# Two-block model at sequence 512: work moved ahead of waits in three stages, and the last product written out in column halves

## The reference, cut to what matters

```python
# second block; the first block (chunked attention, convolution, gates) comes before it
h = h + mixer_ab(rmsnorm(h))                     # layer 0: sparse attention and gated linear attention
h = h + square(relu(rmsnorm(h) @ w_up[0])) @ w_down[0]
h = h + mixer_c(rmsnorm(h))                      # layer 1: stick-breaking attention
h = h + square(relu(rmsnorm(h) @ w_up[1])) @ w_down[1]

def mixer_c(n):                                  # 8 heads of width 128
    q, k, v = split(n @ w_in, (1024, 1024, 1024))
    q, k = rmsnorm(q) * gq, rmsnorm(k) * gk
    return stick_breaking(q, k, v) @ w_out

def stick_breaking(q, k, v):
    z = q @ k.T * d ** -0.5                      # mask: key earlier than query
    lo = where(mask, log_sigmoid(-z), 0)
    rc = cumsum(lo, reversed)
    a = where(mask, exp(log_sigmoid(z) + rc - lo), 0)
    return a @ v
```

## Time and profile before

| | |
|---|---|
| median of 3 runs | 1573.76 us (1573.63 to 1574.47) |
| profiled execution, whole | 1573.52 us |
| profiled execution, first to last instruction (span) | 1571.7 us |
| TensorE busy | 1557.9 us, 99% |
| VectorE busy | 1033.1 us, 66% |
| ScalarE busy | 725.2 us, 46% |
| GpSimd busy | 682.2 us, 43% |
| memory traffic | 92 GB/s over the span |

### The profile page before, as it was taken

One profiled execution on the slowest core, in us unless ns is written; L12 is line 12 of the kernel. 1 busy time (PEld: TensorE's weight loads), 2 busy tenths in 40 slices (PEclk: granted clock), 3 DMA queues, 4 the chain that ended last, 5 costly groups with the idle time before them and its releaser, 6 DMA issues.

```text
span 1571.7 us, 20555 instructions
## 1 busy us (share of the span) xinstructions
PE 1557.9 (99%) x7578; PEld 1279.2 (81%) x7578; DVE 1033.1 (66%) x1342; ACT 725.2 (46%) x1086; POOL 682.2 (43%) x668
## 2 busy tenths in 40 slices
PE   9999999999999999999999999999999999999999
PEld 7888787788778998788888888887887888888887
DVE  7424554674688977558484857878777557575848
ACT  6323433325245565345353535476765453444433
POOL 0002110104345453286675748353333484857564
PEclk9999999999999999999999999999999999999999
DMA  7232222232221221422323131222121314141421
GB/s 247 81 107 80 80 80 80 96 107 80 85 76 55 70 79 57 159 81 103 112 80 135 56 134 53 81 81 81 54 81 45 144 54 161 54 161 54 137 78 54
DMA packets 25731, 145.07 MB, mean 92 GB/s; under 512 B 3936, under 2 KB 5680, under 8 KB 9264
## 3 DMA queue, kind: packets, MB, share of 16 engines
q1 hardware_dynamic: 25648, 143.95, 26.5%
HBM read 141.84 MB, written 2.10 MB: 92 GB/s over the span
## 4 chain that ended last, share of the span: by engine, by line
PE 83%; DVE 11%; ACT 3%; issue 1%; POOL 1%; DVEq 0%; ACTq 0%; POOLq 0%
PE ps_G L614 19%; PE ps_G L616 18%; PE ps_G L615 18%; PE ps_C L1274 5%; PE ps_C L1276 5%; PE ps_C L1275 5%; DVE wide L2666 1%; DVE top L2662 1%; PE ps_AV L1103 1%; PE ps_AV L1274 1%; PE ps_AV L1276 1%; PE ps_AV L1275 1%; DVE wide L2858 1%; PE ps_C L713 1%; DVE tmp L2295 1%
## 5 line engine op out<-in xcount | busy, mean ns | idle before, releaser
L614 PE MATMUL ps_G<-ch,wh 128*128 128x512 f32 x800 | 318.7, 398 | 0.7 <-DVE cl L2326 0.5
L616 PE MATMUL ps_G<-ch,wl 128*128 128x512 f32 x800 | 311.7, 390 | 0.0
L615 PE MATMUL ps_G<-cl,wh 128*128 128x512 f32 x800 | 311.6, 389 | 0.0
L614 PE MATMUL ps_G<-nh,wh 128*128 128x512 f32 x504 | 199.8, 396 | 0.4 <-DVE h L2534 0.2
L2990 DVE TENSOR_TENSOR wl<-raw,wh 128x1024 fp32r<-128x1024 f32 (+1 forms) x104 | 179.2, 1741 | 30.7 <-ACT wh L1923 25.1
L616 PE MATMUL ps_G<-nh,wl 128*128 128x512 f32 x504 | 196.4, 390 | 0.0
L615 PE MATMUL ps_G<-nl,wh 128*128 128x512 f32 x504 | 196.2, 389 | 0.0
L614 PEld LDWEIGHTS ps_G<-ch,wh 128*128 128x128 f32 x800 | 150.2, 188 | 39.4 <-issue 7.1
L615 PEld LDWEIGHTS ps_G<-cl,wh 128*128 128x128 f32 x800 | 150.3, 188 | 33.0 <-issue 2.9
L616 PEld LDWEIGHTS ps_G<-ch,wl 128*128 128x128 f32 x800 | 150.2, 188 | 31.6
L2261 DVE TENSOR_TENSOR wl<-raw,wh 128x2048 fp32r<-128x2048 f32 x45 | 105.1, 2336 | 61.6 <-ACT wh L1416 58.5
(11 more groups left out here) (442 smaller groups left out, 3188.6 us busy)
## 6 DMA issues: line engine op xcount, KB each, us to landing
raw<-wst SPq DMA_DIRECT2D x96, 1024.0 KB, 4.9
raw<-quart_d SPq DMA_DIRECT2D x16, 1024.0 KB, 4.9
tabs<-quart_d SPq DMA_DIRECT2D x8, 1024.0 KB, 6.9
mixed_buffers<-quart_d SPq DMA_DIRECT2D x8, 1024.0 KB, 4.9
raw<-wst SPq DMA_DIRECT2D x8, 256.0 KB, 6.3
out<-wide SPq DMA_DIRECT2D x8, 256.0 KB, 2.0
h<-xT SPq DMA_DIRECT2D x7, 256.0 KB, 6.7
raw<-wst SPq DMA_DIRECT2D x2, 512.0 KB, 5.4
```

Source lines behind the costliest of these rows:

```text
L614: mm(o, ah, bh, start=first, stop=False)
L615: mm(o, ah, bl, start=False, stop=False)
L616: return mm(o, al, bh, start=False, stop=last)
```

## The change

1. In the last group, the block k = 3 of `outc` becomes `fourth`, with bank C1 of its own (the output of head 19 moves to bank ST). All six standing chunks of k = 1 now stand ahead of the turns of head 18, and chunks 0 to 3 of `third` and of `fourth` between the turns of heads 18 and 19. After the heads' outputs come `third` 4 and 5, chunk 6 of blocks 0 and 1, `fourth` 4 and 5, chunk 7 of blocks 0 and 1, and `third` and `fourth` 6 and 7.
2. In group 1, ScalarE does head 13's softplus in its two parts around block 2's evacuation and ahead of the root, and turns out head 13 ahead of the next root. VectorE does the first part of head 13's weights ahead of the Newton step. TensorE's statistic in block 2 moves from chunk 1 to chunk 3.
3. In the first stick blocks, the turns come ahead of chunk 2, the norm's statistic after chunk 6 instead of 5, and VectorE's second piece of the third tile is cut in two, the last quarter after GpSimd's first squares.
4. The last product's second token block is done in two column halves, the second in a fresh bank (SX), with a 256-column add of the older sum in bank C1 put earlier on VectorE and two stores instead of one.

```diff
-                for hd in (prev, prev + 1):
-                    book(("C0", "C1")[hd - prev], ("av", hd))
+                book("C0", ("av", prev))
+                book("C1" if prev == 10 else "ST", ("av", prev + 1))
...
         book("C2", ("third",))
+        book("C1", ("fourth",))
...
+                    if name == "stick":
+                        project_some(so_, 1, oh, ol, standing, True, False)
+                        do_turns(0)
+                        pe.wait_ge(third_lo, 1)
+                        for key in (("third",), ("fourth",)):
+                            take(key)
+                            part_block(so_, key, range(KC // 2))
+                        do_turns(1)
+                        do_av(0, prev)
+                        do_av(1, prev + 1)
+                        need_tile(so_, 1)
+                        part_block(so_, ("third",), (4, 5))
+                        both(c, False)
+                        part_block(so_, ("fourth",), (4, 5))
+                        both(c + 1, True)
+                        return
...
-                    if name == "outc" and k == 2:
+                    if name == "outc" and k in (2, 3):
+                        key = (("third",), ("fourth",))[k - 2]
                         take_block(st, k)
-                        third(st, range(KC // 2, KC)).then_inc(done[use[("third",)][0]], 1)
+                        part_block(st, key, (6, 7)).then_inc(done[use[key][0]], 1)
...
-                    block_(2, 1, 0, stat_at(1, ("qk", qk0)))
+                    block_(2, 1, 0, stat_at(3, ("qk", qk0)))
...
+                if g == 1:
+                    softplus(prev + 1, HALVES[0])
+                    evac_qk(2, 2)
+                    softplus(prev + 1, HALVES[1])
+                    rsqrt(("qk", qk0 + 1))
+                    exponential(prev + 1, HALVES[0])
+                    evac_qk(3, 3)
+                    split(st, 2)
+                    exponential(prev + 1, HALVES[1])
+                    values_out(wide[:, 3, :], st, 4, 0)
+                    turn(prev + 1)
+                    rsqrt(("qk", qk0 + 2))
...
-                some((0, 1), range(3))
+                some((0, 1), range(2))
                 pe.wait_ge(acc_added, end.added(6))
                 for f in range(4, KC):
                     pe.wait_ge(h_new, f - 3)
                     turn_back(f, BACK[f])
+                some((0, 1), (2,))
...
-                some((0, 1), (4, 5))
+                some((0, 1), (4, 5, 6))
                 norm_and_token_stat(4)
-                some((0, 1), (6, 7))
+                some((0, 1), (7,))
...
-                    tt(wl[s][:, 4:8, :], raw[s][:, 4:8, :], wh[s][:, 4:8, :].bitcast(F), ALU.subtract).then_inc(w_lo, 1)
+                    tt(wl[s][:, 4:6, :], raw[s][:, 4:6, :], wh[s][:, 4:6, :].bitcast(F), ALU.subtract)
+                    dve.wait_ge(sq_low, 1)
+                    tt(wl[s][:, 6:8, :], raw[s][:, 6:8, :], wh[s][:, 6:8, :].bitcast(F), ALU.subtract).then_inc(w_lo, 1)
...
+                        for n, (y, bank) in enumerate(LAST_HALVES):
+                            dve.wait_ge(half_done, pt.half(6, 1) + n)
+                            to = accumulator(1, 1)[:, y]
+                            tt(to, to, ps[bank or X[1]][:, y], ALU.add).then_inc(acc_added, 1)
```

More of the change, by code:

```diff
@@ L583, in _ @@
                     store(b, n)
[L584 to L587, removed]
+            for n, (b, y) in enumerate(((0, slice(0, S)), (1, slice(0, TW)), (1, slice(TW, S)))):
+                sp.wait_ge(acc_added, end.added(6) - 1 + n)
+                sp.dma_start(out[b * P:(b + 1) * P, S + y.start:S + y.stop], accumulator(b, 1)[:, y]).then_inc(stored, 16)
+            sp.wait_ge(stored, 16 * (KC + 1))
         @block.tensor
@@ L1038, in _, with part_block @@
                             last.then_inc(done[use[key][0]], 1)
-            def third(st, chunks):
-                s, o = st.slot(1), bank_of(("third",))
+            def part_block(st, key, chunks):
+                s, o = st.slot(1), bank_of(key)
+                col = slice(0, P) if key == ("third",) else slice(P, 2 * P)
                 for c in chunks:
-                    ins = three(o[:], wh[s][:, c, 0:P], wl[s][:, c, 0:P], oh[:, c, :], ol[:, c, :], c == 0, c == KC - 1)
+                    ins = three(o[:], wh[s][:, c, col], wl[s][:, c, col], oh[:, c, :], ol[:, c, :], c == 0, c == KC - 1)
                 return ins
@@ L1138, in attention_group, with both @@
                         do_scores(1)
-                    early = 4 if name == "dsa" else 2
-                    project_some(so_, 1, oh, ol, standing[:early], True, False)
-                    do_turns(0)
[L1142 to L1146, removed]
+                    c = OUT_CHUNK(prev)
+                    def both(c, last):
+                        mixed(c)
+                        for k in range(2):
+                            project_some(so_, k, oh, ol, [c], False, last)
+                    if name == "stick":
[14 more added lines that the diff above has]
+                        return
+                    project_some(so_, 1, oh, ol, standing[:4], True, False)
+                    do_turns(0)
+                    project_some(so_, 1, oh, ol, standing[4:], False, False)
                     do_turns(1)
@@ L1268, in product, with chunk_ @@
                 bh, bl = product_weight(wh[s]), product_weight(wl[s])
-                def chunk_(c, b):
+                def chunk_(c, b, y=slice(0, S), bank=None):
                     x = slice(b * P, (b + 1) * P)
                     ah, al = ring_hi[:, RING[i], c, x], ring_lo[:, RING[i], c, x]
[L1273 to L1276, removed]
+                    o = ps[bank or banks[b]][:, y]
+                    mm(o, ah, bh[:, c, y], start=(fresh or bank is not None) and c == 0, stop=False, skip_group_check=True)
+                    mm(o, ah, bl[:, c, y], start=False, stop=False, skip_group_check=True)
+                    return mm(o, al, bh[:, c, y], start=False, stop=c == 3, skip_group_check=True)
                 if by_block:
-                    for b in range(2):
-                        for c in range(4):
[L1281 to L1285, removed]
+                    for c in range(4):
+                        if c % 2 == 0:
+                            pe.wait_ge(half_lo, pt.half(i, c // 2))
+                        need(c)
+                        ins = chunk_(c, 0)
+                    ins.then_inc(half_done, 1)
+                    for y, bank in LAST_HALVES:
+                        for c in range(4):
+                            ins = chunk_(c, 1, y, bank)
                         ins.then_inc(half_done, 1)
@@ L1330, in layer @@
                                 settled(pe, ("third",))
+                                settled(pe, ("fourth",))
                             turn_h(2 * k)
@@ L2528, in part @@
                             hk = chunk(h, i * 4 + k)
-                            if name == "outc" and k == 2 and not whole:
-                                ready(dve, ("third",))
-                                moved_use(tt(hk, hk, bank_of(("third",))[:], ALU.add), ("third",))
+                            if name == "outc" and t and not whole:
+                                key = (("third",), ("fourth",))[c]
+                                ready(dve, key)
+                                moved_use(tt(hk, hk, bank_of(key)[:], ALU.add), key)
                                 dve.sem_inc(moved[f"G{st.bank(k)}"], 1)
@@ L2910, in attention_group, with tile_and_first_half @@
                 if not soft and g == 1:
+                    def tile_and_first_half():
+                        split(st, 1)
+                        weights(prev + 1, part=0)
                     apply(0)
-                    apply(1, lambda: split(st, 1))
-                    weights(prev + 1)
+                    apply(1, tile_and_first_half)
+                    weights(prev + 1, part=1)
                     output(prev)
@@ L3064, in layer @@
                     half_of(6, 0)
+                    if f and pt.last:
+                        dve.wait_ge(half_done, pt.half(4, 1))
+                        to, (y, _) = accumulator(1, 1), LAST_HALVES[1]
+                        tt(to[:, y], to[:, y], ps[X[1]][:, y], ALU.add)
                     add_up(4, X, 1, 1)
```

23 lines of the change are left out of this document (10 added, 13 removed).

## The result

| | before | changed |
|---|---|---|
| median | 1573.85 us of 15 runs (1573.42 to 1575.79) | 1576.52 us of 15 runs (1576.04 to 1578.39) |
| profiled execution, span | 1571.7 us | 1574.7 us |
| TensorE busy | 1557.9 us | 1558.9 us |

The ratio is 1.0018, with an interval of 1.0010 to 1.0025: 2.7 us slower, where 1574.8 us was forecast in a range of 1572.4 to 1577.4 us. It is inside the range, but 1.7 us above the forecast, and the granted clock fell, which the prediction had named as a sign that it is wrong.

The account below looks back on a forecast made before the run. TensorE, busy 1557.9 of 1571.7 us, was taken as the bound. Terms -0.9 - 1.8 + 4.0 - 0.3 = +1.0 us gave 1574.5 us against the profiled execution, 1574.8 us as median, range 1572.4 to 1577.4 us.

Parts of the forecast that it names:

- Last group: Last group: 24 more matmuls ahead of block 0's last matmul, less old waits, start k = 4 later: +4.0 us.
- The new wait for bank C2: Between head 18's turns and `third`: TensorE waits for ScalarE's copies, 0.95 us, 1.1 us with refill and semaphore.
- the chain from block 0's last matmul: Last group: VectorE and ScalarE work without slack, so k = 4 starts 9.67 us after block 0's last matmul.
- The pause: Ahead of k = 4 in the last group: TensorE stands still about 4.5 us in one piece.
- The clock falls in the new pause: Rival, at k = 4: matmuls behind the pause run at 1.2 GHz, +1.5 us, giving 1576.3 us; chance 0.2.
- the prediction's own last sentence: Wrong if the pause ahead of k = 4 is under 3 us, the granted clock falls, or group 1 shows new waits.
- Group 1: Group 1: waits of 0.85 and 0.73 us go, the statistic's wait moves to the next one: -1.8 us.
- that rival: Group 1 wins nothing: the old 0.85 us wait stays and others follow, 1.8 us lost, 1576.6 us; chance 0.15.
- First stick blocks: First stick blocks: turns 0.1 us, norm's statistic 0.3 us and cut of VectorE's operation 0.5 us, together -0.9 us.
- The third term: First stick blocks: cutting VectorE's operation brings the head statistic forward, gain 0.5 us with refill, bounds 0.3 and 0.6.
- End: Last product in column halves: matmuls +0.16 us, narrower last add -0.3 us, smaller last store -0.15 us; -0.3 us.
- The faster rival: Last group: chain does not hold k = 4, -1.4 us in place of +4.0, time 1569.4 us; chance 0.1.

Follow-up runs that it names:

- e1: Part 1 of the change (last group) alone, against the kernel before: 1580.66 us, ratio 1.0039, +6.2 us.
- e4: Changed kernel with the tile of k = 4 copied and subtracted earlier, ahead of block 1's low part; against the kernel before: 1572.53 us, ratio 0.9985.
- e6: Changed kernel with chunks 6 and 7 of blocks 0 and 1 ahead of chunks 4 and 5 of `third` and `fourth`; against the kernel before: 1574.83 us.
- e3: Changed kernel with 18 additional unread matmuls right ahead of k = 4, keeping TensorE busy; against the kernel before: 1575.45 us, ratio 1.0005.
- e5: Part 2 of the change (group 1) alone, against the kernel before: 1572.05 us, ratio 0.9985, -2.1 us.
- e11: Part 3 without the cut of VectorE's piece (turns and statistic alone), against the kernel before: 1575.42 us in one run.
- e8: Part 3 of the change (first stick blocks) alone, against the kernel before: 1574.12 us in one run.
- e12: Part 4 of the change (column halves at the end) alone, against the kernel before: 1573.63 us, ratio 0.9994, -0.5 us.
- e9: e7 with VectorE adding `third` behind the early tile's subtraction instead of ahead of it; against the kernel before: 1569.05 us, ratio 0.9966, -5.1 us.
- e7: Changed kernel with e4 and e6 together and block 1's chunks 4 and 5 behind head 18's turns; against the kernel before: 1571.64 us, ratio 0.9982.
- e2: Parts 2 to 4 of the change, last group as before; against the kernel before: 1571.67 us, ratio 0.9981, -2.8 us.

## Why the prediction was right, and where it was off

**Last group: mechanism and size right.** Forecast +4.0 us; k = 4 came at 1217.28 us against 1215.55 us, while the same trace had been 2.1 us ahead at the head of the group: +3.9 us, and +3.9 us in e1. The new wait for bank C2 was priced at 1.1 us with its refill, and its bracket alone is 1.11 us. e4 and e6 show that the chain from block 0's last matmul sets the start: cut by 3.0 us or begun 2.5 us sooner, it moved k = 4 with it. The pause was put at about 4.5 us and is 4.56 us; all the standing still behind block 0 was put at some 6 us, and the three brackets (0.19, 0.56 and 4.56 us) are 5.3 us.

**The clock: the rival that came true.** "The clock falls in the new pause", given 0.2 and +1.5 us, happened, at +1.7 us in the profiled execution. It is the distance between the forecast and the result, because the errors of the other terms nearly cancel: 0.4 us too much for the first stick blocks, 0.2 to 0.3 us too little for group 1. e3 shows it by taking the pause away and leaving the chain. All fifteen runs of the changed kernel had a mean clock of 0.999 or 0.998, the latter seven at 1576.77 us or more. The step that failed is the sum, which held the clock at nothing, and the 0.2 for this rival behind it: that no row showed the lower level was no evidence that a pause four times the longest of the earlier trace rows would leave the clock alone. With the rival's 1.5 us in the forecast the sum is 1576.3 us. By the prediction's own last sentence the fall of the clock makes it wrong here; the time lies in the range because the range had been drawn wide enough for most of this rival, and not because the sum held.

**Group 1: right, a little small.** -1.8 us forecast; -2.0 us in the trace, -2.1 us in e5. Both waits went and the remaining one moved to 1058.75 us as said, so that rival falls.

**First stick blocks: too large.** -0.9 us forecast, -0.5 us in the trace. The 0.3 us of the statistic and the 0.1 us of the turns, held down by the tile's new wait of 0.35 us, are there (0.6 us together in e11). The third term, 0.5 us for the cut of VectorE's piece, rests on the sentence that VectorE does the held half "in about 0.6 us while TensorE does the statistic". It took 1.51 us, because it ran into GpSimd's next square. That TensorE would not wait for it was the step that failed in this term: it waited 0.75 us.

The Trainium skill's rule of an exclusive lock, from the page "SBUF — State Buffer", section "SBUF: two separate sides", was weighed for the square that the cut freed, and not for the one that the held quarter would meet. There, by an estimate from that rule and e8's rows, the quarter would wait 0.96 us for the square's end and work 0.68 us, 1.64 us in all; 1.51 us is measured. For the first square this rule would give 0.6 us, and 0.53 us is measured (1.78 to 1.25 us). The traces agree with it nearly, not to the last tenth.

**End: -0.3 us forecast.** e12 gives -0.5 us with an interval that holds no change, so only the sign is likely. The additions of 0.42 us stand at the end of the trace as said.

**The faster rival** would have needed a k = 4 that does not wait for blocks 0 and 1, and even to break even one within 8.7 us of block 0's last matmul. It came after 9.67 us in both kernels.

## What to carry to other kernels

Work moved ahead of a wait is only free if it isn't moved ahead of the start of the next chain. Find the last matmul that the coming chain needs, count what you put ahead of it, and what is left behind it to cover the chain; the cure (e9) was to order by that matmul and to shorten the chain, and it turned +2.7 into -5.1 us. If a new pause of some microseconds is unavoidable, price the slower clock behind it as part of the pause. And when an operation is cut so that its second half runs later, look at which engine's work it will meet there.

## What was not expected of the hardware

How long the clock stays down varies from run to run, and how long a pause brings it down isn't one number here. Pauses ahead of k = 4 (each from the one trace of its kernel), and the runs' mean clocks:

| kernel | pause | mean clock of the runs | lost behind the pause in the trace |
|---|---|---|---|
| e9 | 0.30 us | four of 5 at 1.000 | none |
| e4 | 1.60 us | 11 of 11 at 1.000 | none |
| e7 | 2.00 us | 5 of 11 at 1.000, the others 0.999 | 1.7 us |
| e6 | 3.15 us | 1 of 11 at 1.000, the others 0.999 or 0.998 | 2.9 us |
| e1 | 4.55 us | none of 5 at 1.000 | 2.8 us |
| changed | 4.56 us | none of 15 at 1.000 | 1.7 us |

e7's runs at 1.000 took 1570.41 to 1571.33 us, those at 0.999 1571.64 to 1572.86 us. In the four traces with a fall the lower level lasted 3.4 us (changed, e7) or 6.8 us (e1, e6), and TensorE lost about half of the part that met its matmuls. The fall came 1.1 us (e1) and 0.7 us (e6) ahead of k = 4, and 0.1 us (changed) and 0.8 us (e7) behind its start. What decides within one kernel isn't settled.

The clock also fell where TensorE hardly waited, in stages that no kernel here changes: in e2's profile at 482 us, behind a stretch of small matmuls (26 in the window of 2 us).

```profile
478.00:480.00 2.00, 2.00 (x26) 1.00 0.05 12
...
482.00:484.00 2.00, 2.00 (x6) 0.56 0.00 0
484.00:486.00 2.00, 2.00 (x5) 0.59 0.00 0
486.00:488.00 2.00, 2.00 (x11) 1.00 0.80 213
```

e11's profile has the same at 404 us. Of the 69 later runs of the kernel before, 8 show a clock of 0.999; they took 1575.74 to 1576.36 us, some 1.7 us over the median of the others. Those runs left no trace, so where the clock fell in them isn't shown. It is part of the scatter of this kernel, and a reason not to read a difference of 2 us from single runs.
